# Gates by exponential, add and reciprocal instead of a sigmoid activation, in one layer of a hybrid encoder

## The reference

```python
q_lat, c_kv, k_r, f_q, f_k, f_v, f_logit, m_q, g = jnp.split(h @ w_in, split_points, axis=-1)
...
gates = jax.nn.sigmoid(g.astype(jnp.float32)).astype(h.dtype).reshape(b, s, N_BRANCH, D_MODEL)
...
y = (gates[:, :, 0] * (o_mla.reshape(b, s, -1) @ w_br_mla)
     + gates[:, :, 1] * (o_fox.reshape(b, s, -1) @ w_br_fox)
     + gates[:, :, 2] * (o_mem.reshape(b, s, -1) @ w_br_mem))
return y @ w_out
```

## Time and profile before

| | |
|---|---|
| time, median of 3 runs | 1287.64 us (1286.06 to 1288.28) |
| the profiled execution, its own time | 1288.28 us |
| its span, first to last instruction | 1286.5 us |
| TensorE busy | 1221.3 us (95%) |
| VectorE busy | 537.5 us (42%) |
| ScalarE busy | 200.3 us (16%) |
| mean granted TensorE clock | 0.973 |

### The profile page before, as it was taken

The page is one execution under the profiler, slowest core; times in us unless marked ns, Lnnn a source line. Parts: engine busy times, 40 slices in busy tenths (PEclk is TensorE's granted clock), DMA queues, the critical chain, the costliest instruction groups (busy, mean ns, idle before and its releaser), DMA issues.

```text
span 1286.5 us, 17492 instructions
## 1 busy us (share of the span) xinstructions
PE 1221.3 (95%) x6418; PEld 674.5 (52%) x6418; DVE 537.5 (42%) x1475; ACT 200.3 (16%) x368; POOL 44.1 (3%) x53
## 2 busy tenths in 40 slices
PE   7789999999999999989879999999999999999994
PEld 4345445555565665434645555555555555555541
DVE  1221003343565563333534544445544445544436
ACT  1101212333422220001100001110001110101113
POOL 0100000000000000000010000000000000000000
PEclk9899999999999999999679999999999999999998
DMA  8150145220264455783414999999999999999981
GB/s 283 67 179 24 43 153 162 82 72 35 92 209 128 130 194 193 273 323 116 137 30 173 382 391 376 381 384 369 383 390 375 380 381 383 387 393 375 371 359 52
DMA packets 82293, 309.00 MB, mean 240 GB/s; under 512 B 13920, under 2 KB 19456, under 8 KB 56128
## 3 DMA queue, kind: packets, MB, share of 16 engines
q1 hardware_dynamic: 67136, 275.01, 54.8%
q0 software_dynamic: 5696, 15.47, 4.1%
q10 hardware_dynamic: 9408, 17.83, 4.0%
HBM read 302.25 MB, written 10.74 MB: 243 GB/s over the span
## 4 chain that ended last, share of the span: by engine, by line
PE 92%; DVE 5%; DMA 2%; issue 1%; ACT 0%; ACTq 0%; SPq 0%; DVEq 0%
PE ps_P L1173 18%; PE ps_P L909 10%; PE ps_V L1198 9%; PE ps_V L1187 9%; PE ps_P L815 7%; PE ps_S L1187 4%; PE ps_T L808 4%; PE ps_P L823 3%; PE ps_V L1126 3%; PE ps_V L1117 3%; PE ps_T L1162 3%; PE ps_P L1067 2%; DMA small<-gates 2%; PE ps_S L918 2%; PE ps_V L1150 1%; PE ps_P L1050 1%
## 5 line engine op out<-in xcount | busy, mean ns | idle before, releaser
L1173 PE MATMUL ps_P<-arena,branch_out 128*64 128x256 f32 (+1 forms) x2176 | 233.6, 379 | 0.5 <-DVE branch_out L1783 0.5
L1173 PEld LDWEIGHTS ps_P<-arena,branch_out 128*64 128x64 f32 (+1 forms) x2176 | 151.3, 135 | 90.7 <-issue 19.1
L909 PE MATMUL ps_P<-weight_ring,xT 128*128 128x512 f32 x288 | 136.2, 600 | 0.0
L1789 DVE TENSOR_TENSOR branch_out<-branch_out,ps_P 128x256 f32<-128x256 f32 x33 | 13.9, 421 | 266.2 <-PE ps_P L1173 266.2
L1187 PE MATMUL ps_V<-weight_ring,branch_out 128*128 128x512 f32 x264 | 124.2, 593 | 0.0
L1198 PE MATMUL ps_V<-arena,branch_out 128*64 128x512 f32 (+1 forms) x544 | 120.6, 599 | 0.0
L1350 ACT ACTIVATE weight_ring<-ps_V,merge 128x512 f32<-128x512 f32 x66 | 45.3, 687 | 427.5 <-PE ps_V L1198 427.5
L1810 DVE TENSOR_TENSOR x_sb<-x_sb,ps_V 128x512 f32<-128x512 f32 x136 | 93.6, 688 | 23.0 <-PE ps_V L1187 17.3
L1187 PEld LDWEIGHTS ps_V<-weight_ring,branch_out 128*128 128x128 f32 x264 | 48.1, 192 | 47.3 <-issue 47.3
L909 PEld LDWEIGHTS ps_P<-weight_ring,xT 128*128 128x128 f32 x288 | 50.5, 191 | 40.8 <-issue 40.3
L1187 PE MATMUL ps_S<-weight_ring,branch_out 128*128 128x512 f32 x132 | 67.4, 593 | 0.0
(11 more groups left out here) (306 smaller groups left out, 1325.4 us busy)
## 6 DMA issues: line engine op xcount, KB each, us to landing
arena<-w_e_gate SPq DMA_DIRECT2D x68, 1024.0 KB, 8.7
arena<-w_e_up SPq DMA_DIRECT2D x68, 1024.0 KB, 10.5
arena<-w_e_down SPq DMA_DIRECT2D x68, 1024.0 KB, 7.2
weight_ring<-w_in SPq DMA_DIRECT2D x12, 1024.0 KB, 8.2
weight_ring<-w_in ACTq DMA_DIRECT2D x8, 1024.0 KB, 6.2
gates<-arena ACTq DMA_DIRECT2D x18, 256.0 KB, 3.4
small<-gates ACTq DMA_DIRECT2D x18, 256.0 KB, 4.0
arena<-cache_fox_k SPq DMA_DIRECT2D x8, 512.0 KB, 4.0
```

The costliest lines, as they stand in the source:

```text
L909: last = mm(out[:, :], xT[:, k, j * P:(j + 1) * P], slot[:, k % 4, :], start=(k == 0), stop=(k == KD - 1))
L1173: last = mm(bank[r:r + wide, 0:256], xgT[q][:, k, r:r + wide], w[h][:, k, :], start=(k == 0), stop=(k == KD - 1))
```

## The change

The gate's activation on ScalarE becomes exp(-g) instead of sigmoid(g). VectorE gets a part in the step `("P", "g", m)`: it waits until ScalarE has evicted the tile, adds 1 to `estage` in place, takes the reciprocal in place, and increments the new semaphore `gate_ready`. The store of the gate waits for `gate_ready` instead of ScalarE's own eviction. 1/(1 + exp(-g)) is the sigmoid. Nothing else is changed.

```diff
@@ -513,6 +513,7 @@
         gates_stored = sem("gates_stored")
+        gate_ready = sem("gate_ready")
@@ -1241,7 +1242,7 @@
                 n = gates["stored"]
                 if n < gates["made"]:
-                    act.wait_ge(free["P"], done_at("P", "g", n))
+                    act.wait_ge(gate_ready, n + 1)
                     act.dma_start(gates_dram[n], estage).then_inc(gates_stored, 16)
@@ -1286,7 +1287,7 @@
                             act.wait_ge(gates_stored, 16 * n)
-                        last = fn(estage, src[:, :], ACT.Sigmoid)
+                        last = fn(estage, src[:, :], ACT.Exp, scale=-1.0)
                         gates["made"] += 1
@@ -1620,6 +1621,12 @@
                     last.then_inc(free["T"], 1)
+                elif ring == "P" and key[0] == "g":
+
+                    dve.wait_ge(free["P"], done_at(*st))
+                    e = estage
+                    link(V.tensor_scalar(e, e, 1.0, None, ALU.add))
+                    V.reciprocal(e, e).then_inc(gate_ready, 1)
                 elif ring == "rms":
```

## The result

The changed kernel takes 1325.08 us (median of 4 runs, 1320.33 to 1329.11) against 1287.96 us before: ratio 1.029, 95% interval 1.0254 to 1.0325. The sign was right. The size was not: 1389 us was forecast, and the range ended at 1354. The profiled execution took 1329.72 us, 1327.9 us of span, 41.4 us more than the span before; it is the slowest of the five on record, so what its trace shows adds up to some 4 us more than the medians differ by.

The account below looks back on a forecast made before the run. TensorE's never-idle queue was taken to bound attention, so delays to it are paid in full. Stalls of 70.0 us plus clock dips of 30.6 gave 100.6 us on 1288.28, so 1389 us, range 1354 to 1415.

Parts of the forecast that it names:

- The sign: Whole kernel: slower by more than 0.2%, chance 0.97; faster 0.02, within it 0.01.
- E + 4.71: Release of scores n+1, counted from E, the start of TensorE's next instruction after the gate's last matmul.
- 0.11 us: TensorE's start after VectorE's last instruction where it waited for a bare increment, read at a memset; taken as 0.10.
- The second term: Clock: one dip to half clock behind each of 18 waits, 18 x 1.70 = 30.6 us; bounds 0 and 61.
- 1.70 us: Full-clock time lost per dip, taken from the one behind TensorE's 2.80 us idle at the stage's entrance.
- The table loads on the path: ScalarE in attention: 35 loads go, 44.9 us, all beside TensorE's matmuls, worth 0 on its path.
- The reciprocal by two rows: VectorE's reciprocal at 512 columns, from the rows at one and 192 columns: 3.35 us.
- The cover h: TensorE's work between a gate and the next scores, hiding part of the wait: 16.19 us over seventeen gates.
- the 65.6 us of stalls: TensorE waiting at the scores behind seventeen gates: 17 x 4.81 - 16.19, 3.86 us each on average.
- The last gate: Eighteenth gate, no scores behind it: norm(62), a copy and transposes follow its reciprocal, 4.4 us later.
- no second wait follows: After each wait VectorE catches up: some 1.6 us of its work against over 3 us of TensorE's.
- a wait that mostly hides: Rival: reciprocal at its 1.35 us lower bound, waits 1.9 us each, 34 us, clock holds: 1322 us; chance 0.05.

Follow-up runs that it names:

- the kernel with the extra wait: Changed kernel plus a VectorE wait for gate_ready behind the gate's reciprocal, before norm(n-1): 1397.78 us, 1.0861 of before.
- the kernel with the increment first: Changed kernel with the increment of free["S"] moved ahead of the gate's wait on VectorE: 1327.83 us, 1.0313 of before.

## Why the prediction was wrong

**The step that failed** is the end of the sum "3.35 reciprocal: the increment comes at E + 4.71": that the bare increment of free["S"] waits for the end of the reciprocal ahead of it. That TensorE's scores for unit n+1 need exactly this increment was right, its place in the queue too, and the lengths in the sum within 0.07 us. But VectorE's queue went on while the reciprocal ran, and so the increment left before E + 1.47, where the scores started in the timeline around the fourth gate, 3.17 us ahead of the reciprocal's end. The extra wait puts it back: scores at E + 4.87, and 1397.78 us against 1325.08. The prediction took its 0.11 us for such an increment from the earlier trace rows, where a `link` on the memset had made the queue wait for the end. That row priced another case.

The Trainium skill (VectorE: DVE Perf Modes, Two Vector instructions with no wait between them) counts a semaphore operation among the instructions that the sequencer handles alone. By that rule the trace agrees.

**What came in its place** is shorter. The scores, 0.4 to 2.3 us long, and for most units of the new stream a gate piece of 1.72 us run beside the reciprocal. TensorE waits up to 0.9 us for the early increment, and then again, for up to 1.9 us (3.9 at the last gate), where it needs norm(n-1) or a copy. In the profiled execution its waits in attention are 26.1 us in sum, where 70.0 were forecast. That the two waits of a gate don't add up is shown by the kernel with the increment first.

**The clock.** The second term was mis-sized too. In the kernel with the extra wait each of the seventeen waits, those of 2.2 and 2.3 us behind the second and the eleventh gate included, brought a loss in the next iteration: 1.5 to 1.6 us in seven places, 2.6 to 3.3 in ten, mean 2.4. So a dip behind waits of this length was right, and its 1.70 us was the price of the shorter kind only. In the changed kernel all waits but the last are below 2 us, and the clock stays at 1.00 from 230 to 470 us. The two windows of 0.89 show dips that did come, 30 x 0.11 = 3.3 us of full clock in each, and another at the last gate lost 1.7 (a clock of 0.83 from 530 to 540 us): some 8 us, where 30.6 were forecast. The length of one wait does not tell whether a dip comes: the waits of 1.88 us behind the thirteenth and the fourteenth gate brought none, and the dips of the two windows came beside waits of 0.98 and 1.25 us, behind the sixteenth and the seventeenth. What decides it is left open here. Why the changed kernel's times spread over 9 us is not settled either: its executions with shorter spans had a higher mean clock (1318.5 us with 0.973, 1327.9 with 0.965), which fits a varying number of dips.

**Point by point.** The table loads on the path: forecast 0, measured 0.9991 of before, right. The reciprocal by two rows, 3.35 us: 3353 ns, right. The cover h was misread in two places: in iterations 7 and 39 another gate piece stands behind the gate's last, so E was taken 1.72 us late and the cover 1.72 us too short. With 3.4 us less, the 65.6 us of stalls become 62.2, and the kernel that has them measured 63.3. The last gate: forecast 4.4 us, 3.94 us of wait measured, the dip not counted. That "no second wait follows" was wrong for the changed kernel, since behind the early increment the second wait is the one that counts; in the kernel with the extra wait it held. The rival "a wait that mostly hides" (0.05, 1322 us) came nearest in time, but its mechanism, a reciprocal of 1.35 us, is not what happened: it hides behind scores that were let go early. The range was too narrow because the order of the increment was taken as certain and had no bound of its own.

## What to carry to other kernels

In a kernel where one engine is never idle, price new work on another engine by the longest block that stands ahead of something that engine needs, not by its sum: 68 us of VectorE work cost 37, 17 or 7 us by its place and cut. Before a wait is put on a path, look at who sends the increment: here one attached to the reciprocal came at its end, and a bare one behind it came 3.17 us earlier, when the queue got there. An increment that has to mean "done" needs to be attached, or to stand behind a wait, as in the kernel with the extra wait. Fewer table loads were worth nothing here, where the engine that pays for them waits for others anyway.

## What the runs showed of the hardware that was not expected

A bare increment in VectorE's queue let TensorE start 3.17 us before the instruction ahead of it ended. VectorE's float32 reciprocal took 1208 ns at 170 columns, 1354 at 192 and 3353 at 512, about 6.25 ns more per column. Tanh and Exp alternated without any table load between them, and the gate's activation took 597 ns with Sigmoid, Exp and Tanh alike.
